# One output projection of a two-layer decoder step: block products with weight sums made by adding transfers

## The reference

```
def pool_mixer(h, prefix, qpos, w_in, w_grp, pool_scale, w_out):
    u, z = jnp.split(h @ w_in, 2, axis=-1)
    ...
    mixed = jnp.einsum('btgc,gcd->btgd', pooled, w_grp).reshape(B, T, D_POOL)
    y = mixed * pool_scale * jax.nn.silu(z)
    return y @ w_out, u_ext[:, -POOL_BUF:]
...
    x = x + gate * y
```

## Time and profile before

| | us |
|---|---|
| median of 3 runs | 2404.41 |
| lowest, highest | 2403.69, 2404.58 |
| profiled execution | 2407.84 |
| its span, first to last instruction | 2406.2 |
| TensorE busy in the span | 2351.2 |
| vector engine busy | 1179.1 |
| scalar engine busy | 824.6 |
| GpSimd busy | 350.3 |

### The profile page before, as it was taken

How to read it: one execution, slowest core, us unless ns; L and a number is a source line. 1 busy time by engine, 2 the same in 40 slices (tenths; PEclk the granted TensorE clock), 3 DMA queues, 4 the chain that set the end, 5 groups by cost and what they waited for, 6 DMA issues and landing times.

```text
span 2406.2 us, 48916 instructions
## 1 busy us (share of the span) xinstructions
PE 2351.2 (98%) x20327; PEld 2216.9 (92%) x20327; DVE 1179.1 (49%) x2057; ACT 824.6 (34%) x1383; POOL 350.3 (15%) x509
## 2 busy tenths in 40 slices
PE   7999999999999999999989999999999999998997
PEld 6988988898999999999989999999989988878997
DVE  1236111222164345333487777777666666654343
ACT  1125121112142233111354444444455545543222
POOL 2002000593000000110110000000033323323000
PEclk9999999999999999999999999999999999999998
DMA  9985887576644435773444444444533333497222
GB/s 337 354 292 189 273 251 249 187 235 214 218 150 136 138 105 178 229 243 124 124 109 132 132 132 132 132 132 132 154 106 105 106 89 97 147 379 270 88 88 89
DMA packets 400917, 419.69 MB, mean 174 GB/s; under 512 B 21734, under 2 KB 353766, under 8 KB 398322
## 3 DMA queue, kind: packets, MB, share of 16 engines
q1 hardware_dynamic: 384610, 349.70, 46.0%
q0 software_dynamic: 16112, 67.14, 8.3%
HBM read 383.59 MB, written 55.27 MB: 182 GB/s over the span
## 4 chain that ended last, share of the span: by engine, by line
PE 93%; DVE 3%; ACT 1%; issue 1%; DMA 0%; POOL 0%; SPq 0%; ACTq 0%; DVEq 0%; POOLq 0%
PE acc L2473 44%; PE acc L2624 19%; PE acc L2651 8%; PE work L2388 4%; PE work L2677 3%; PE work L2328 3%; PE out_acc L2714 2%; PE work L2745 1%; PE acc L2328 1%; PE acc L2699 1%; PE work L2376 1%; PE acc L2758 1%; PE acc L2821 1%; PE out_acc L2709 1%; PE work L2668 1%
## 5 line engine op out<-in xcount | busy, mean ns | idle before, releaser
L2473 PE MATMUL acc<-h_hi,w_hi 128*128 128x260 f32 x2832 | 581.7, 287 | 2.5 <-DVE w_lo L1576 1.9
L1576 DVE TENSOR_TENSOR w_lo<-raw,w_hi 128x1024 fp32r<-128x1024 f32 (+1 forms) x220 | 272.7, 1240 | 624.1 <-ACT w_hi L1139 623.9
L2473 PE MATMUL acc<-h_hi,w_lo 128*128 128x260 f32 x2832 | 571.1, 283 | 0.0
L2473 PE MATMUL acc<-h_lo,w_hi 128*128 128x260 f32 x2832 | 570.1, 283 | 0.0
L1139 ACT ACTIVATE w_hi<-raw 128x1024 fp32r<-128x1024 f32 (+1 forms) x220 | 231.0, 1051 | 785.5 <-PE acc L2473 775.1
L2473 PEld LDWEIGHTS acc<-h_hi,w_hi 128*128 128x128 f32 x2832 | 436.3, 189 | 29.0 <-issue 27.6
L2473 PEld LDWEIGHTS acc<-h_hi,w_lo 128*128 128x128 f32 x2832 | 437.3, 189 | 0.0
L2473 PEld LDWEIGHTS acc<-h_lo,w_hi 128*128 128x128 f32 x2832 | 436.9, 189 | 0.0
L1909 DVE TENSOR_TENSOR block_lo<-block,block_hi 128x1024 fp32r<-128x1024 f32 x168 | 205.4, 1224 | 106.9 <-ACT block_hi L1381 106.8
L1381 ACT ACTIVATE block_hi<-block 128x1024 fp32r<-128x1024 f32 x168 | 177.6, 1058 | 191.2 <-DVE block L1944 64.5
L2624 PE MATMUL acc<-t_hi,block_hi 128*128 128x260 f32 x768 | 217.3, 283 | 3.5 <-DVE block_lo L1909 2.1
(11 more groups left out here) (415 smaller groups left out, 3487.6 us busy)
## 6 DMA issues: line engine op xcount, KB each, us to landing
ada<-in_w_ada SPq DMA_DIRECT2D x192, 512.0 KB, 4.8
block<-in_w_in_b SPq DMA_DIRECT2D x96, 512.0 KB, 4.6
raw<-in_w_in_a SPq DMA_DIRECT2D x64, 512.0 KB, 5.0
raw<-in_w_kv SPq DMA_DIRECT2D x48, 512.0 KB, 3.6
raw<-in_w_out_a SPq DMA_DIRECT2D x32, 512.0 KB, 3.5
raw<-in_w_in_b SPq DMA_DIRECT2D x32, 512.0 KB, 4.5
raw<-in_w_out_b SPq DMA_DIRECT2D x32, 512.0 KB, 3.6
pages_early<-in_cache_k_cmp SPq DMA_DIRECT2D x32, 256.0 KB, 4.3
```

The source lines that it names most:

```text
L1576: V.tensor_tensor(LO[j % 2][:, :, 0:n], RAW[j][:, :, 0:n], HI[j % 2][:, :, 0:n].bitcast(F32), ALU.subtract).then_inc(lo_ready, 1)
L2473: last = mm_(out[half][0:n, 0:HT], part[slot][:, kk, cols_], src[:, k, half * HT:(half + 1) * HT], start=(first and part is HI and src is ...
```

## The change

The first and the last of the eight pairs stay as they are. The six between them (`A_PAIR`) become seven products each (`A_PROD`), in the order P1, P4, P2, P7, P5, P6, P3. A product multiplies a weight block of 1024 rows by 128 columns, 512 KB, with a block of y of 1024 rows by 260 columns: 24 matmuls. The blocks of y are y itself for P1, P2 and P3 and four sums of blocks of y for the others. Three of these sums the vector engine forms in place in `Y`, the fourth is an adding transfer inside SBUF; their high and low parts go to `TH_A` and `TL_A`. Four of the weight blocks are sums as well. GpSimd forms them with transfers that add onto their destination, after the remainder of what was there has been taken:

- after P1: a block from HBM is added onto P1's buffer, for P7 (A in what follows)
- after P4: a block from HBM onto P4's buffer, for P5 (B)
- after P7: another block from HBM onto P7's buffer, for P6 (C)
- after P2, and when the one before has landed: P6's buffer onto P2's buffer, for P3 (D)

P1's buffer alternates between raw0 and raw3; the other two, raw1 and raw2, serve all pairs. The four bias tables are issued behind the fourth of these transfers in the first four of the six pairs. Two rows of x come back later, since their place holds copies of products. TensorE starts a product when the high part of its weights is there and waits for the low part behind 16 of the 24 matmuls. The rest of the diff shifts counts of semaphores in later stages.

```diff
+A_P1, A_P4, A_P2, A_P7, A_P5, A_P6, A_P3 = range(A_PROD)
...
+def a_block(p):
+    i, s = divmod(p, A_PROD)
+    x = 3 * (i % 2)
+    return (x, 1, 2, x, 1, x, 2)[s]
...
@@ SP @@
-            quads(Q_OA, w_oa, 8)
+            quads(Q_OA, w_oa, 1)
...
+            def a_free(i, buffer):
+                last = A_PROD * (i - 1)
+                if buffer in (0, 3):
+                    if i > 1:
+                        sp.wait_ge(lo_ready, a_count(last - A_PROD + A_P6))
+                        sp.wait_ge(sums_in[2], a_summed(last - A_PROD + A_P3))
...
+                elif i:
+                    sp.wait_ge(lo_ready, a_count(last + (A_P5 if buffer == 1 else A_P3)))
...
+            for i in range(A_PAIR):
+                for buffer in (3 * (i % 2), 1, 2):
+                    a_free(i, buffer)
+                    a_load(i + 1, buffer)
...
@@ GpSimd @@
+            pool.wait_ge(s_pooled, 7)
+            pool.dma_start(Y[:, 8:KT, 0:HT], Y[:, 8:KT, HT:T], accum_op=ALU.add).then_inc(s_x1[3], 16)
...
+            def a_sum(buffer, src):
+                pool.dma_start(by_cols(RAW[buffer]), src, accum_op=ALU.add).then_inc(sums_in[buffer], 16)
...
+            for i in range(A_PAIR):
+                p, x = A_PROD * i, 3 * (i % 2)
+                pool.wait_ge(lo_ready, a_count(p + A_P1))
+                a_sum(x, a_src(i, 0, P))
+                pool.wait_ge(lo_ready, a_count(p + A_P4))
+                a_sum(1, a_src(i, 0, P))
+                pool.wait_ge(lo_ready, a_count(p + A_P7))
+                a_sum(x, a_src(i, 8, P))
+                pool.wait_ge(sums_in[x], a_summed(p + A_P6))
+                pool.wait_ge(lo_ready, a_count(p + A_P2))
+                a_sum(2, by_cols(RAW[x]))
+                if i < NH // 4:
+                    bias_table(i)
+            pool.wait_ge(s_ute, 4 + 2 * A_PAIR)
+            x_back(14, 2)
...
@@ scalar engine @@
+                nc.scalar.activation(by_cols(HI[p % 2]), by_cols(RAW[buffer]), ACT.Copy).then_inc(hi_ready, a_step(p))
...
+            hi(Q_OA, 1)
+            t_hi_a(0)
+            hi(Q_OA, 2)
+            t_hi_a(1)
+            t_hi_a(2)
+            hi(Q_OA, 3)
+            t_hi_a(3)
+            a_hi(0)
+            for p in range(A_PROD * A_PAIR):
+                i, s = divmod(p, A_PROD)
+                if p + 1 < A_PROD * A_PAIR:
+                    a_hi(p + 1)
...
+                if s in (A_P1, A_P7, A_P5):
+                    act.wait_ge(w_used, a_count(p))
...
+                    nc.scalar.activation(copy[:, :], bank[:, 0:HT], ACT.Copy).then_inc(st_copied, 1)
+                if s in (A_P4, A_P5):
+                    square_a(2 * i + (s == A_P5))
...
@@ vector engine @@
+                elif s == A_P6:
+                    dve.wait_ge(st_copied, 3 * q + 3)
+                    V.tensor_tensor(P1A[:, :], D[3][:, 0:HT], P1A[:, :], ALU.subtract).then_inc(st_added, 1)
+                    dve.wait_ge(st_added, 5 * q + 2)
+                    o(V.tensor_tensor(P5A[:, :], P1A[:, :], P5A[:, :], ALU.subtract))
+                    V.tensor_tensor(U2A[:, :], U2A[:, :], P1A[:, :], ALU.subtract).then_inc(st_added, 1)
+                    V.tensor_tensor(P1A[:, :], D[2][:, 0:HT], P1A[:, :], ALU.add).then_inc(st_added, 1)
+                    row_add(row + 1, 1, P5A)
+                    dve.wait_ge(st_added, 5 * q + 4)
+                    row_add(row + 1, 0, P1A).then_inc(s_ute, 1)
...
+            turn_a(0, {1: lambda: (t_sum_a(0), t_sum_a(1)), 2: lambda: (t_sum_a(2), t_lo_a(1)), 3: lambda: t_lo_a(0), 0: lambda: a_lo(0),
+                       "between": lambda: t_lo_a(3)})
+            for p in range(A_PROD * A_PAIR):
+                i, s = divmod(p, A_PROD)
+                if p + 1 < A_PROD * A_PAIR:
+                    a_lo(p + 1)
...
+                if s in (A_P2, A_P6, A_P3):
+                    a_out(p)
+                if s in (A_P4, A_P5):
+                    square_sum_a(2 * i + (s == A_P5))
...
@@ TensorE @@
-            pairs(Q_OA, D_OA, 8, (ys, 0))
+            for j in range(4):
+                quad(Q_OA, D_OA, j, (ys, 0))
...
+                if s == A_P1:
+                    pe.wait_ge(acc_free, 2 * D_OA + 1)
+                    wait(pe, st_added, 5 * (i - 1) + 1 if i else 0)
...
+                pe.wait_ge(hi_ready, a_count(p))
+                for kk in range(8):
+                    for part, b in enumerate((b_hi, b_lo)):
+                        mm_(out[:, 0:HT], w_hi[:, kk, :], b[:, k0 + kk, at:at + HT],
...
+                pe.wait_ge(lo_ready, a_count(p))
+                for kk in range(8):
+                    last = mm_(out[:, 0:HT], w_lo[:, kk, :], b_hi[:, k0 + kk, at:at + HT], start=False, stop=(kk == 7), skip_group_check=True)
...
+            for p in range(A_PROD * A_PAIR):
+                a_product(p)
+            pe.wait_ge(st_added, A_ADD)
+            for j in range(4):
+                quad(Q_A7, D_A7, j)
```

More of the change, by code:

```diff
@@ L508, in build @@
         s_rows = sem("setup_rows_in")
[L509 to L510 removed]
+        s_x = [sem(f"x_rows_then_a_sums{3 * i}_in") for i in range(2)]
+        s_rel = sem("rel_then_a_sums1_in")
         dve_set = sem("dve_set")
@@ new lines, in a_lo, with row_add @@
+            def a_lo(p):
+                dve.wait_ge(hi_ready, a_count(p))
+                V.tensor_tensor(by_cols(LO[p % 2]), by_cols(RAW[a_block(p)]), by_cols(HI[p % 2]).bitcast(F32),
+                                ALU.subtract).then_inc(lo_ready, a_step(p))
+            def row_add(row, half, src):
+                gate = MODT[:, 2 * KT + row, :]
+                x, at = X[:, row, :], half * HT
+                n = HT if half == 0 else HT - TS
+                last = V.scalar_tensor_tensor(out=x[:, at:at + n], in0=src[:, 0:n], scalar=gate[:, 0:1], in1=x[:, at:at + n], op0=ALU.mult, op1=ALU.add)
+                if half:
+                    rt = RT[row % 2]
+                    o(V.tensor_tensor(rt[:, :], src[:, n:HT], gate[:, 1:NC], ALU.mult))
+                    last = V.tensor_tensor(x[:, TP:T], x[:, TP:T], rt[:, :], ALU.add)
+                return last
@@ new lines, in a_out @@
+            def a_out(p):
+                q, s = divmod(p, A_PROD)
+                row = 2 * (q + 1)
+                dve.wait_ge(w_used, a_count(p))
+                if s == A_P2:
+                    dve.wait_ge(s_x1[row // 4], 32 if row == 12 else 16)
+                    row_add(row, 0, D[0][:, 0:HT]).then_inc(st_added, 1)
+                elif s == A_P6:
[8 more added lines that the diff above has]
+                    row_add(row + 1, 0, P1A).then_inc(s_ute, 1)
+                elif s == A_P3:
+                    V.tensor_tensor(U2A[:, :], D[1][:, 0:HT], U2A[:, :], ALU.add).then_inc(st_added, 1)
+                    dve.wait_ge(st_added, 5 * q + 5)
+                    row_add(row, 1, U2A).then_inc(s_ute, 1)
@@ L2367, in stat @@
                 for half in range(2):
-                    last = mm_(((S if r else D)[half])[:, 0:HT], ones, (SUM if r else SUM0)[:, half * HT:(half + 1) * HT], start=True, stop=True)
+                    last = mm_(((S if r else D)[half])[:, 0:HT], ones, (SUMA if r else SUM0)[:, half * HT:(half + 1) * HT], start=True, stop=True)
                 last.then_inc(stat_done, 1)
```

292 lines of the change are left out of this document (223 added, 69 removed).

## The result

The changed kernel takes 2467.49 us (median of 4 runs, 2465.91 to 2468.54), beside 2404.49 us of the kernel before in the same set of runs: 1.026 times as long, 95% interval 1.0243 to 1.0278. The forecast was slower, 2456 us in a range of 2402 to 2510. The profiled execution took 2468.54 us with a span of 2466.9 us, 60.7 us over that of before.

A forecast was written before the change was run, and what follows sets the result against it. TensorE, busy 98% of the span, was taken as the bound. Terms 28.7 + 0.7 + 3.5 + 1.9 + 11.9 + 4.8 = +51.5 us on 2404.41 gave 2456 us, range 2402 to 2510.

The forecast's parts named there:

- pairs, without tables: Six pairs, a first of 26.6 us and five of 28.1: 167.1 against 138.4 us, +28.7 us.
- clock: TensorE's clock falls once per pair and once on the way in: 7 x 1.7 = +11.9 us.
- bias tables: Behind D in pairs 1 to 4, a table delays the load for the next P2: 4 x 1.2 = +4.8 us.
- quads, and wait going in: Before the pairs: quad 3's remainder late, +0.7 us; P1 waits behind the adding transfer on y, +3.5 us.
- output add in front of the last pair: The plain pair at the end waits for the last output add on the vector engine: +1.9 us.
- The price of an adding transfer: Weight sums in each pair: 6.8 us for A, B and C from HBM, 5.1 for D inside SBUF.
- moving twice: Adding transfers read the destination too: fixed 2.4 us plus twice the 2.2 us of moving, for A to C.
- The rivals with 3.8 us and with 9.2 us: A to D cheap as the quickest load, 2395.5 us, chance 0.14; each add two transfers long, 2505 us, chance 0.20.
- The sum of y: Adding transfer on y blocks before the pairs, priced by x coming back: 7.8 us, between 5.1 and 10.2.
- a P6 that runs slow is hidden while D moves: In each pair, P6 at the lower clock is hidden during transfer D; no size given.
- the table is over: In the pairs, at the forecast's price the pair is so long that the 16.1 us table ends before the next A.
- the signs announced: Next profile: waits before P6 and P3, D about 5 us, pairs 27 to 30 us, 144 matmuls fewer, clock under 1.

The follow-up runs named there:

- tables one by one: Changed kernel with its bias tables moved behind the pairs, one ahead of each of the second to fifth group of kv rows: 2446.85 us, ratio 1.0172.
- extra matmuls: Against the kernel with tables in the kv stage and y's sum on the vector engine: 20 unread matmuls before P6, 14 before P3; 2435.58 us, ratio 1.0122.
- twin: Changed kernel with bias tables one at a time in the kv stage and y's fourth sum on the vector engine: 2438.17 us, ratio 1.0138.

## Why the prediction was right, and where it was not

The direction and the cause held: seven products save 17.3 us only if the sums arrive in time, and the chain of two adding transfers in each pair does not let them. The kernel with the vector engine's sums shows the saving, the one with plain transfers how much hangs on the price of the transfers. By the forecast's own terms:

| term | forecast, us | measured, us | from |
|---|---|---|---|
| pairs, without tables | +28.7, clock apart | +30.6, clock included | 169.0 - 138.4, tables one by one |
| clock | +11.9 (7 x 1.7) | 1.8 in six pairs, within the line above | extra matmuls, twin, both without tables |
| bias tables | +4.8 | +20.6 | tables one by one |
| quads, and wait going in | +0.7 + 3.5 | +6.2 | start of P1 |
| output add in front of the last pair | +1.9 | +2.3 | its wait |
| sum | +51.5 | +60.7 span, of which the lines hold 59.7; +63.0 median | |

- **The price of an adding transfer** was right. Forecast 6.8 us for A to C and 5.1 for D; in the changed kernel A to C took 6.2 to 7.6 us with no table in flight, and D, in four pairs just ahead of one, 4.5 to 6.0. The queue's rows bear out moving twice: the engines are occupied for 4.3 us by an adding C (forecast 4.4), and for 2.8 against 1.3 us by D. The rule of the Trainium skill (Collectives: The Full Stack, The bandwidth ceiling: the fold count and why AG ≠ RS ≠ AR), stated there for a ring of several cores, points the same way. The rivals with 3.8 us and with 9.2 us are out.
- **The sum of y** took 10.2 us, its upper bound, not 7.8, and the wait going in was 5.5 us instead of 3.5. The forecast priced it by x coming back, which the trace shows as 128 packets of 8320 bytes, 0.39 us each; the sum of y goes in 1024 packets of 1040 bytes, 0.124 us each. That is 3.1 and 7.9 us on each of 16 engines, 2.5 times as much, not twice. The same neighbours in the queue, the copy of the pooling state and four rows of a bias table, stood behind both.
- **The pairs**: 28.2 us in the mean without tables, forecast 26.6 and five times 28.1. The single waits agree less well than their sum: before P3 0 to 3.3 us, by how slow the P6 before it ran and how long D took, and P1 never waited for its remainder, where 0.7 was forecast.
- **The clock** was the first term that failed. It fell in every pair, as forecast, but where extra matmuls could test it, in the kernel without tables in the pairs, 1.8 of 10.2 us lie on the path. The forecast itself says that a P6 that runs slow is hidden while D moves, and then counted one fall a pair all the same; in that kernel five of six falls are of that kind. In the changed kernel it is one of six pairs: P3 runs slow in pairs 1 to 3 and P2 behind a table's wait in pairs 2 to 5, and P1, going in, takes 4.83 instead of 3.06 us. What these falls cost, no run separates.
- **The bias tables** were the second: 4.8 forecast, 20.6 measured. I had taken the landing times of before, 11.5 and 8.9 us, for the new order. But beside A, B and twice as many transfers the load that P2 waits for landed after 12.7 to 13.9 us, not 9.5, and P2 waited 3.6 to 6.9 us instead of 2.5. The forecast also held that at this price "the table is over" when the next A is issued. Its own times speak against that: a table that goes out behind D, at about 19 us of the pair, and takes 16.1 lasts to 35, and the next A goes out at 28.1 + 2.7 = 30.8. A and B of pairs 2 to 5 needed 11.4 to 13.8 us.
- These two errors, 10.1 us too much and 15.8 too little, cancel in good part: that the forecast's total lies only 9.2 us under the measured growth of the span is luck, its parts are worse.
- Of the signs announced, 144 matmuls fewer, waits before P6 and P3 in most pairs, D at about 5 us, the clock under 1 and unchanged later stages were found; pairs of 27 to 30 us were not (30.4 to 32.8 but for the last, 27.6), for the tables.

## What to carry to other kernels

A product form that saves matmuls is worth what its operand sums cost on the path: with a pair of 20 us, two dependent transfers of 6.8 and 4.6 us between a remainder and a copy undid it, and adds of 1.2 us on an engine that had just enough room for them (109.6 of 123.75 us busy) made it pay. Work that "only moves" to another place in a queue, like the four tables, must be priced against the loads in flight there: a stage that loads just in time paid 11 us a table, one that loads ahead hid them one by one. When an edit leaves the total alone, compare the time at a stage's boundary first: 19 us were won and lost again here.

## What the runs showed of the hardware

- A copy of 1 MB from HBM to HBM slows the transfers of other queues too: SP's plain loads of 512 KB from 5 us to between 12 and 19, GpSimd's adding ones from 6.5 to between 11 and 15, whether GpSimd or the scalar engine had issued it, while with the table alone in flight the DMA engines were busy at 0.23.
- An adding transfer of 512 KB inside SBUF occupies the 16 DMA engines 2.1 times as long as a plain one in as many packets (2.8 and 1.3 us). GpSimd issues it in 0.89 instead of 0.56 us, and one from HBM, where the plain one has fewer packets, in 1.54 instead of 0.88.
- A GpSimd add of 1024 columns out of SBUF holds up vector instructions with both operands in SBUF until it ends (8 columns: 2.34 instead of 0.16 us), and is held up by them (2825 instead of 2386 ns); a vector add with one operand in PSUM took its usual 0.49 us beside one.
- TensorE at the lower clock in front of a wait cost little: 0.91 and 1.00 of granted clock differed by 1.8 us in 165.
